# Two transformer blocks on one core: angles moved to GpSimd, the FFN's second half interleaved, and one half of a weight split per latent attention item

## The reference

```python
def _swiglu(h, w_in, w_out):                      # four times: FFN 0 to 3, inner width 2816
    gate, up = jnp.split(h @ w_in, 2, axis=-1)
    return (jax.nn.silu(gate) * up) @ w_out

def _rope(x, positions):                          # cos and sin of angles up to some 1280
    ang = positions.astype(jnp.float32)[..., None] * inv_freq
    cos, sin = jnp.cos(ang), jnp.sin(ang)
    ...

for li in range(DEPTH):                           # DEPTH = 2
    x = x + 0.5 * _swiglu(_rmsnorm(x, g[0]), ffn_w_in[li, 0], ffn_w_out[li, 0])
    ...                                           # li 0: gated linear attention; li 1: latent attention, 16 heads
    x = x + 0.5 * _swiglu(_rmsnorm(x, g[2]), ffn_w_in[li, 1], ffn_w_out[li, 1])
    gate = jax.nn.sigmoid((_rmsnorm(x, g[3]) @ ple_w_gate[li]).astype(jnp.float32))
    x = x + (gate * (p[li] @ ple_w_in[li]))
    # after li 0: the latent keys and values, ckv = rmsnorm(x @ kv_w_down), k_rope = _rope(...)
# second block, per layer:  mod = silu(c) @ w_ada[l] + b_ada[l]   (1024 x 3072, needed long after the FFNs)
```

## Time and profile before

| what | value |
|---|---|
| median of 3 runs (1601.73 to 1613.8) | 1607.42 us |
| the profiled execution's own time | 1614.45 us |
| its span | 1612.6 us |
| TensorE matmul, busy share | 95% |
| VectorE, ScalarE, GpSimd, busy share | 69%, 48%, 11% |
| `w_hi` of a half (L646), mean | 1040 ns x452 |
| `w_lo` of a half (L1674), mean | 1248 ns x452 |
| one part of modulation (L1706), mean | 614 ns x112 |
| GpSimd's issue of one modulation DMA (L531), mean | 540 ns x128 |

### The profile page before, as it was taken

The page is one execution under the profiler, slowest core; times in us unless marked ns, Lnnn a source line. Parts: engine busy times, 40 slices in busy tenths (PEclk is TensorE's granted clock), DMA queues, the critical chain, the costliest instruction groups (busy, mean ns, idle before and its releaser), DMA issues.

```text
span 1612.6 us, 31237 instructions
## 1 busy us (share of the span) xinstructions
PE 1528.2 (95%) x12299; PEld 1468.0 (91%) x12299; DVE 1107.4 (69%) x1659; ACT 779.7 (48%) x1259; POOL 184.7 (11%) x224
## 2 busy tenths in 40 slices
PE   7999998989999989999999999999997999989998
PEld 6999998989999989999989799999997976889767
DVE  5886559965886577875676746975588458394583
ACT  5554374454543456443453635543464338253481
POOL 1111015501111010111010001111023000020000
PEclk9999999999999999999999999999998999999999
DMA  7787644425776645776645154876644613075010
GB/s 223 239 264 241 219 131 131 124 75 162 234 251 215 219 130 174 248 224 197 205 121 151 52 165 153 273 235 194 209 149 140 172 41 105 1 228 174 21 53 26
DMA packets 219308, 264.85 MB, mean 164 GB/s; under 512 B 22253, under 2 KB 197325, under 8 KB 219213
## 3 DMA queue, kind: packets, MB, share of 16 engines
q1 hardware_dynamic: 209136, 234.58, 46.6%
q0 software_dynamic: 8960, 27.37, 5.2%
q10 hardware_dynamic: 1117, 1.57, 0.3%
HBM read 262.44 MB, written 1.05 MB: 163 GB/s over the span
## 4 chain that ended last, share of the span: by engine, by line
PE 70%; DVE 15%; ACT 6%; DMA 6%; issue 3%; POOL 0%; DVEq 0%; SPq 0%; ACTq 0%
PE bank L1006 20%; PE bank L1008 20%; PE bank L1007 20%; DVE w_lo L1674 6%; DMA mod_raw<-in_w_ada 3%; PE bank L1574 2%; ACT w_hi L646 1%; DMA w_raw<-in_ffn_w_in 1%; PE bank L1413 1%; PE bank L1607 1%; DVE rs L1686 1%; ACT xh L657 1%; DVE hg_s L1902 1%; ACT sq L664 1%; DVE mod_acc L1706 1%
## 5 line engine op out<-in xcount | busy, mean ns | idle before, releaser
L1006 PE MATMUL bank<-xh,w_lo 128*128 128x256 f32 x2312 | 653.3, 283 | 25.3 <-DVE xl L2157 13.5
L646 ACT ACTIVATE w_hi<-w_raw 128x1024 fp32r<-128x1024 f32 x452 | 454.4, 1040 | 438.8 <-PE bank L1008 279.0
L1674 DVE TENSOR_TENSOR w_lo<-w_raw,w_hi 128x1024 fp32r<-128x1024 f32 x452 | 547.9, 1248 | 153.7 <-ACT w_hi L646 152.5
L1007 PE MATMUL bank<-xl,w_hi 128*128 128x256 f32 x2312 | 648.5, 280 | 0.0
L1008 PE MATMUL bank<-xh,w_hi 128*128 128x256 f32 x2312 | 648.3, 280 | 0.0
L1006 PEld LDWEIGHTS bank<-xh,w_lo 128*128 128x128 f32 x2312 | 439.6, 190 | 30.2 <-DVE xl L2157 14.5
L1007 PEld LDWEIGHTS bank<-xl,w_hi 128*128 128x128 f32 x2312 | 439.4, 190 | 1.1 <-issue 0.7
L1008 PEld LDWEIGHTS bank<-xh,w_hi 128*128 128x128 f32 x2312 | 437.5, 189 | 0.2
L1006 PE MATMUL bank<-hh,w_lo 128*128 (+1 forms) x704 | 197.3, 280 | 5.8 <-DVE w_lo L1674 5.8
L1007 PE MATMUL bank<-hl,w_hi 128*128 (+1 forms) x704 | 196.4, 279 | 0.0
L1008 PE MATMUL bank<-hh,w_hi 128*128 (+1 forms) x704 | 196.4, 279 | 0.0
(11 more groups left out here) (365 smaller groups left out, 2185.1 us busy)
## 6 DMA issues: line engine op xcount, KB each, us to landing
w_raw<-in_ffn_w_in SPq DMA_DIRECT2D x176, 512.0 KB, 4.7
w_raw<-in_ffn_w_out SPq DMA_DIRECT2D x88, 512.0 KB, 4.4
w_raw<-in_w_in SPq DMA_DIRECT2D x52, 512.0 KB, 4.7
mod_raw<-in_w_ada POOLq DMA_DIRECT2D x128, 192.0 KB, 4.3
w_raw<-in_a_w_in SPq DMA_DIRECT2D x32, 512.0 KB, 4.5
w_raw<-in_ple_w_gate SPq DMA_DIRECT2D x16, 512.0 KB, 4.3
w_raw<-in_b_w_out SPq DMA_DIRECT2D x16, 512.0 KB, 4.2
w_raw<-in_w_out SPq DMA_DIRECT2D x16, 512.0 KB, 3.6
```

What stands on the lines that cost most here:

```text
L646: A(w_hi[:, c % NSLOT, cols], w_raw[:, c % NRAW, cols], ACT.Copy).then_inc(*did(hi_ready))
L1006: mm(out, lhs[1], rhs[0], start=start, stop=False, skip_group_check=skip)
L1007: mm(out, lhs[0], rhs[1], start=False, stop=False, skip_group_check=skip)
L1674: V.tensor_tensor(w_lo[:, c % NSLOT, cols], w_raw[:, c % NRAW, cols], f32(w_hi[:, c % NSLOT, cols]), ALU.subtract).then_inc(*did(lo_ready))
```

## The change

It has four parts.

1. **Angles to GpSimd.** VectorE keeps only the first instruction (the angle out of PSUM). The rest becomes 14 instructions on GpSimd in three groups, `turns_of_angles` (3), `reduce_angles` (7) and `quarter_turn` (4), placed between modulation DMAs of FFN 1, after blocks 1, 2 and 3. The multiply-and-add that VectorE did in one instruction is two there, and the absolute value is maximum minus minimum. The sines move on ScalarE to the second half of FFN 1 (`before_out`, behind `hi` of out chunk 7), and the sign goes to GpSimd behind the last modulation DMA. VectorE waits for `rope` in FFN 2.
2. **The FFN's second half interleaved.** `lo` and `hi` of out chunks 4 to 12 are written out, without a loop; block 6 of modulation stands behind `lo` of out chunk 4, block 7 behind that of 6. `before_out` is called in two pieces, behind chunks 5 and 7. This holds for all four FFNs.
3. **Latent attention.** Each item from 0 to 7 has one half of a chunk to split instead of each of items 4 to 7 having two. On ScalarE it stands at the item's end, behind `oh`.
4. On ScalarE the loads of `load_late` in FFN 0 come one chunk later.

The programs of TensorE and SyncE keep their order.

```diff
@@ gpsimd: modulation(f), behind the four DMAs of block k
+                if f == 1 and k == 1:
+                    turns_of_angles()
+                if f == 1 and k == 2:
+                    reduce_angles()
+                if f == 1 and k == 3:
+                    quarter_turn()
+
+        def turns_of_angles():
+            pool.wait_ge(*when("ang0"))
+            G.tensor_scalar(turns[:, :], ang[:, :], float(1 / (2 * np.pi)), None, ALU.mult).then_inc(*did(pool_steps))
+            big = float(1.5 * 2 ** 23)
+            for step in (big, -big):
+                pool.wait_ge(*did.last)
+                G.tensor_scalar(turns[:, :], turns[:, :], step, None, ALU.add).then_inc(*did(pool_steps))
+
+        def reduce_angles():
...
+            for part in (part1, part2, part3):
+                pool.wait_ge(*did.last)
+                G.tensor_scalar(mag[:, :], turns[:, :], -part, None, ALU.mult).then_inc(*did(pool_steps))
+                pool.wait_ge(*did.last)
+                G.tensor_tensor(red[:, :], mag[:, :], src[:, :], ALU.add).then_inc(*did(pool_steps))
+                src = red
...
@@ gpsimd, behind modulation(1)
-        pool.wait_ge(*when("rope"))
+        pool.wait_ge(*when("sin"))
+        G.tensor_scalar(sin[:, :], sin[:, :], const[:, C_SIGN:C_SIGN + 1], None, ALU.mult).then_inc(*did(pool_steps, "rope"))
@@ scalar: ffn
             c = first[f"out{f}"]
-            hi(c + NSLOT)
-            if before_out is not None:
-                before_out()
-            with act.Fori(0, 2) as it:
-                for q in range(4):
-                    hi(c + 1 + q + NSLOT, it)
-            did.skip(hi_ready, 8)
+            for q in range(9):
+                hi(c + q + NSLOT)
+                if before_out is not None and q in (1, 3):
+                    before_out(q)
@@ scalar: latent attention
         for i in range(8):
             exps(("b", i), 2 * (i % 2), sB[:, i % 3], nmB[:, i % 3], denB[:, i % 3])
-            if i >= 4:
-                hi(first["bout"] + i - 4)
             if i >= 1:
                 probs_t(("b", i - 1), ptB[:, (i - 1) % 2], 3 * P)
             if i >= 2:
...
+            hi(first["bout"] + i // 2, None, [i % 2])
@@ vector: ffn
-            lo(c + NSLOT)
-            for q in range(2):
-                for part in range(MOD_PARTS):
-                    modulate(f, 6 + q, part)
-            if before_out is not None:
-                before_out()
-            with dve.Fori(0, 2) as it:
-                for q in range(4):
-                    lo(c + 1 + q + NSLOT, it)
-            did.skip(lo_ready, 8)
+            for q in range(9):
+                lo(c + q + NSLOT)
+                if q in (0, 2):
+                    for part in range(MOD_PARTS):
+                        modulate(f, 6 + q // 2, part)
+                if before_out is not None and q in (1, 3):
+                    before_out(q)
@@ vector: angles (all but the first instruction leave)
             V.tensor_scalar(ang[:, :], bank[7][:, 0:T], const[:, C_FREQ:C_FREQ + 1], None, ALU.mult).then_inc(*did(dve_steps, "ang0"))
-            dve.wait_ge(*did.last)
-            V.tensor_scalar(turns[:, :], ang[:, :], float(1 / (2 * np.pi)), None, ALU.mult).then_inc(*did(dve_steps))
...
@@ vector: latent_split (ckl leaves the first piece for the second)
+        def latent_split(q):
+            if q == 3:
+                dve.wait_ge(*when("ckh"))
+                V.tensor_tensor(ckl[:, :, :], ck[:, :, :], f32(ckh[:, :, :]), ALU.subtract).then_inc(*did(dve_steps, "ckl"))
+                return
@@ vector: latent attention
-            if i >= 4:
-                lo(first["bout"] + i - 4)
+            lo(first["bout"] + i // 2, None, [i % 2])
```

More of the change, by code:

```diff
@@ L1961, in _, with embedding @@
             lo(first["aout"] + j + AHEAD)
-        def embedding(l):
-            dve.wait_ge(*when(("ptin", l)))
-            V.tensor_copy(pt[:, :, :], two(bank[2][:, :])).then_inc(*did(dve_steps, ("pt", l)))
-            dve.wait_ge(*when(("pth", l)))
-            V.tensor_tensor(ptl[:, :, :], pt[:, :, :], f32(pth[:, :, :]), ALU.subtract).then_inc(*did(dve_steps, ("ptl", l)))
-        ffn(1, 3, 2, g_norm(0, 2), 2, [first["in1"] - 1 + AHEAD], angles, lambda: embedding(0))
+        def embedding(l, q):
+            if q == 1:
+                dve.wait_ge(*when(("ptin", l)))
+                V.tensor_copy(pt[:, :, :], two(bank[2][:, :])).then_inc(*did(dve_steps, ("pt", l)))
+            else:
+                dve.wait_ge(*when(("pth", l)))
+                V.tensor_tensor(ptl[:, :, :], pt[:, :, :], f32(pth[:, :, :]), ALU.subtract).then_inc(*did(dve_steps, ("ptl", l)))
+        ffn(1, 3, 2, g_norm(0, 2), 2, [first["in1"] - 1 + AHEAD], angles, lambda q: embedding(0, q))
         def ple(l, nu, v, s):
@@ L2024, in latent_split @@
                 V.tensor_tensor(krz[rows_, h, :], kr_t[rows_, 0, :], kr_t[rows_, 1, :], ALU.add).then_inc(*did(dve_steps))
-            dve.wait_ge(*when("ckh"))
-            V.tensor_tensor(ckl[:, :, :], ck[:, :, :], f32(ckh[:, :, :]), ALU.subtract).then_inc(*did(dve_steps, "ckl"))
         ffn(2, 6, 4, g_norm(1, 0), 4, (), latent, latent_split)
```

69 lines of the change are left out of this document (34 added, 35 removed).

## The result

The changed kernel takes 1600.72 us in the median of 20 runs, the kernel before 1611.05 us in 20 runs on the same chip. The ratio is 0.9935, with a 95% interval of 0.9914 to 0.9957: about 10 us faster (7 to 14), where 16.3 was forecast. By the bound of 1% that the prediction set this is "within 1%". The profiled execution took 1599.1 us (span 1597.3), against 1598.2 in the working and 1614.45 for the profiled run of before. That close agreement is partly luck, as the experiments show. The forecast's 1591 stood on three runs of before (median 1607.4); the twenty have 1611.05, so 3.6 of the 9.7 us between 1591 and 1600.7 come from the base and the rest from the gain.

The account below looks back on a forecast made before the run. TensorE, busy 95% of the span, bounds the kernel, so only its waits and low clock matter. Gains 4.7 + 9.0 + 2.6 = 16.3 us take the median from 1607.4 to 1591 us; range 1582 to 1602.

Parts of the forecast that it names:

- the bound of 1%: Whole kernel: about 1%, 16 us, can arise from no change; only below 1591.3 us counts as faster.
- 4.7 + 0.9: FFN 1: 4.7 us from the angles leaving VectorE plus 0.9 us from the reordered second half.
- Angles off VectorE (4.7): FFN 1 after the first pair: TensorE's 2.67 us wait for w_lo and the low clock behind it go, gaining 4.7 us.
- Second halves (9.0): Second halves of all FFNs: waits for w_lo go, gaining 6.1 + 0.9 + 1.5 + 0.5 = 9.0 us.
- The replay: FFN 2's second half on VectorE in the new order: chunks 5, 6, 7 ready with margins 8.7, 7.8 and 3.6 us.
- the price of FFN 2: FFN 2's second half: without the 3.37 us wait, 124 matmuls per 20 us become 179, gaining 6.1 us.
- The new order on ScalarE and the straight code: Second halves of the FFNs: both cost nothing, being covered behind a TensorE that never waits for them.
- Latent attention (2.6): TensorE's two waits for ptB fall from 2.49 and 2.80 to about 0.9 and 1.7 us, gaining 2.6 us.
- it may stay: Latent attention: the low clock following the ptB waits was not counted as gain.
- GpSimd (0, at most 3.8): Angles in FFN 1: no cost at 0.78 us per instruction, at most 3.8 us at 1.35; VectorE splits held up 0.9 each.
- Half of the gain coming back (1599): Rival, 25%: hidden costs on GpSimd (3.8), in attention (4.2) or at chunk 7's margin leave a gain of about 8 us.
- The pace: Rival, 12%: fewer stalls mean more stretches at 179 matmuls in FFN 2 and FFN 3, 7 us more gain: 1584.

Follow-up runs that it names:

- the twins: The changed kernel with the halves of out chunk 3 behind item 7 of latent attention, with angles on GpSimd (1602.0 us) or back on VectorE (1603.45 us).
- before_again: The kernel before, unchanged, in one execution for a second profile; no run time is given.

## Why the prediction was right, and where it was off

To compare stages across profiles, the draws must come out first. I summed, for each stage between its last `X` writes on VectorE, the time in which TensorE's starts were at the wide spacing and took 3.8% of it off. Over the whole span that time is 410 to 715 us, so the draws alone move a run by up to 305 x 0.038 = 12 us. FFN 2 shows that the correction works: its raw lengths with the new order, in the eight profiles without an edit that disturbs it, are 199.0 to 203.4 us; corrected, six of them lie within some 0.3 of 195.2 and the other two at 194.1 and 196.6. Means of the corrected stages, over all profiles whose edit leaves that stage as named (their number in brackets; for FFN 1 the change means both parts that touch it):

| stage | code of before | code of the change | gain | forecast |
|---|---|---|---|---|
| FFN 0 | 202.5 (4) | 201.3 (8) | 1.1 | 0.5 |
| FFN 1 | 189.2 (3) | 183.2 (5) | 6.0 | 4.7 + 0.9 |
| FFN 2 | 197.9 (4) | 195.3 (8) | 2.6 | 6.1 |
| latent attention | 166.3 (4) | 163.4 (6) | 2.9 | 2.6 |
| FFN 3 | 184.4 (4) | 182.8 (8) | 1.6 | 1.5 |

The sum is 14.2 us against 16.3 forecast and 10.3 (7 to 14) by the run times. FFN 0's 1.1 isn't clear of scatter: the four stages with the code of before span 3.4 us by themselves, mostly by the wait at 54 us, which the change doesn't touch. The stages outside the table come out some 0.9 us longer with the changed code, also within their scatter.

- *Angles off VectorE (4.7).* The mechanism was right: the wait went, with the low clock behind it. VectorE's `gate_t` of the second pair came 4.4 us earlier, counted from the start of the stage, where 4.65 was worked out. In the corrected stage the part is worth 4.0 alone (185.2 against 189.2) and 5.6 beside the new second halves (183.2 against 188.8). In the changed kernel's own profile 2 us of the stage's gain went back, since no wait followed at which the spacing could change: FFN 1's loop ran wide where before had drawn narrow, and the raw stage is only 3.4 us shorter, the corrected one 5.5. The timed comparisons (2.9 for it alone, -1.9 by taking it out of the changed kernel, 1.0 between the twins) can't confirm 4 to 5 us, and why they come out lower stays open.
- *Second halves (9.0).* The replay was right to 0.4 us a step, 0.8 at chunk 7, and TensorE waited for none of these chunks. The mis-sized term is the price of FFN 2: "the wait goes: 179 - 124 = 55 matmuls, 6.1 us". Those 55 came from one profile, whose corrected stage is indeed some 6 us longer than the changed code's. Three others with the same code show 152 to 157 matmuls and no fall of the clock, and their stages are only some 1.2 us longer; the mean of all four gives the 2.6. The step took the length of one wait and the clock behind it as the kernel's own, while both went with the spacing at which TensorE came to the place. The new order on ScalarE and the straight code, costed at nothing, were not tried apart; no wait in the second halves speaks against the nothing.
- *Latent attention (2.6).* Waits 0.96 and 1.55 for 0.9 and 1.7, item period 4.82 us as before, so the added halves cost nothing; the stage gained 2.9 us. But the number is partly luck, for the same reason as in FFN 2. The second wait of before, 2.80 us, is 0.96 to 1.13 in the three other profiles with its code, so the 1.1 us taken for it were one profile's: there the change makes that wait longer. `before_again`:

```profile
930.01 0.49 PE L1442 MATMUL bank<-ptB,vb 128*128 128x128 f32 x2 [1.13 <-ACT ptB L891]
```

  In its place came the low clock, left unpriced because "it may stay": in 920 to 940 us the mean is 0.91 in all four profiles with the code of before, and behind the new waits it stays at 1.00 in all six with the changed code.
- *GpSimd (0, at most 3.8).* The cost was 0, but the duration was nearer to the upper end: 16.3 us for the three groups, where 10.8 was taken and 18.8 kept as the end, with single instructions up to 1.71. VectorE was held up far less than the 0.9 us per split that was borrowed from the earlier trace rows: the four pairs of splits beside the angles took 2.62 to 3.10 us, against 2.35. The Trainium skill (SBUF — State Buffer, Who interferes with whom) says that a VectorE instruction with two SBUF inputs contends with a GpSimd instruction that reads SBUF, and calls the shared port pair an exclusive lock. The trace agrees in kind. Read as the prediction read it, each excluding the other for its whole length, the rule would have overpriced this part: the lengthening, 0.2 us per split in the mean, is about a fifth of one GpSimd instruction's 1.16.
- *The rivals.* Half of the gain coming back (1599) is nearest to the median of 1600.7, but not by the causes that it named: neither attention nor GpSimd nor chunk 7 cost anything. The pace didn't rise clearly with fewer stalls: 535 us at the wide spacing in the profile before, 514 after, where single profiles lie between 410 and 715. The forecast's own 1591 lies outside the interval of the difference, the range of 1582 to 1602 held.

So the sign and the mechanisms stood. The size, 16.3, was too large, against 10.3 by the runs and 14.2 by the stages, and the one term that the stages show as clearly too large is FFN 2's. The 4 us between 14.2 and 10.3 reach the edge of the interval, and no experiment here assigns them.

## What to carry to other kernels

Before a wait is priced by the matmuls that a window lacks, look at a second profile of the same kernel. The wait in FFN 2 returned each time here, but its length lay between 1.5 and 3.4 us with the spacing ahead of it, and the low clock came only with the longest; of the two waits in attention the second shrank from 2.8 to 1. Move long chains of small work off the engine that feeds the bound one, and check on the receiving engine what is queued behind them: here a DMA with 8 us to spare for each group. And compare stages, not spans, when parts of a change are worth 2 to 6 us and the runs lie 20 us apart.
